# A hybrid decoder block on one core: down projections two output tiles at a time, alternating between their two banks

## The reference, cut to what matters

```
x   = layer_norm(ALPHA * x + mix, ln1_g, ln1_b)
hid = silu(einsum('bsd,df->bsf', x, w_gate)) * einsum('bsd,df->bsf', x, w_up)
ffn = einsum('bsf,fd->bsd', hid, w_down)          # D_FF = 2816, D_MODEL = 1024
x   = layer_norm(ALPHA * x + ffn, ln2_g, ln2_b)
```

## Time and profile before

| | |
|---|---|
| Time, median of 3 runs | 1458.66 us (1458.49 to 1458.88) |
| Time of the profiled execution | 1459.72 us |
| Its span, first to last instruction | 1457.9 us |
| Mean granted clock of TensorE | 0.996 of full speed |
| TensorE busy | 1438.5 us, 99% |
| VectorE, GpSimd, ScalarE busy | 796.0, 601.2, 485.2 us |

### The profile page before, as it was taken

How to read it: one execution, slowest core, us unless ns; L and a number is a source line. 1 busy time by engine, 2 the same in 40 slices (tenths; PEclk the granted TensorE clock), 3 DMA queues, 4 the chain that set the end, 5 groups by cost and what they waited for, 6 DMA issues and landing times. The chain is left out here.

```text
span 1457.9 us, 19033 instructions
## 1 busy us (share of the span) xinstructions
PE 1438.5 (99%) x6658; PEld 1195.1 (82%) x6658; DVE 796.0 (55%) x1196; ACT 485.2 (33%) x933; POOL 601.2 (41%) x374
## 2 busy tenths in 40 slices
PE   9999999999999999999999899999999999999997
PEld 7888888888888888887887688888888888888886
DVE  3126564557457644766866835545345353454547
ACT  4433433343334323334255332312323223232133
POOL 2221122212312231214873484655637547364464
PEclk9999999999999999999999999999999999999999
DMA  6211111111111011011420121212111112112112
GB/s 174 59 44 44 44 29 58 41 31 43 43 43 43 29 51 50 29 43 58 124 79 15 58 73 37 65 43 65 50 44 58 50 58 64 29 60 61 45 51 116
DMA packets 128407, 80.22 MB, mean 55 GB/s; under 512 B 8433, under 2 KB 123121, under 8 KB 128369
## 3 DMA queue, kind: packets, MB, share of 16 engines
q1 hardware_dynamic: 128368, 79.73, 18.2%
HBM read 75.53 MB, written 4.19 MB: 55 GB/s over the span
## 5 line engine op out<-in xcount | busy, mean ns | idle before, releaser
L1341 PE MATMUL ps<-act_hi,w_hi 128*128 128x512 f32 x864 | 339.3, 393 | 1.1 <-DVE act_lo L906 1.1
L476 POOL TENSOR_TENSOR w_lo<-raw,w_hi 128x1024 fp32r<-128x1024 f32 x54 | 131.6, 2437 | 505.3 <-ACT w_hi L616 505.3
L1342 PE MATMUL ps<-act_lo,w_hi 128*128 128x512 f32 x864 | 337.3, 390 | 0.0
L1343 PE MATMUL ps<-act_hi,w_lo 128*128 128x512 f32 x864 | 337.1, 390 | 0.0
L564 POOL TENSOR_TENSOR w_lo<-raw,w_hi 128x512 fp32r<-128x512 f32 x80 | 108.3, 1354 | 227.8 <-ACT w_hi L819 227.8
L1343 PEld LDWEIGHTS ps<-act_hi,w_lo 128*128 128x128 f32 x864 | 162.6, 188 | 34.5
L1341 PEld LDWEIGHTS ps<-act_hi,w_hi 128*128 128x128 f32 x864 | 162.6, 188 | 33.5 <-issue 1.3
L1342 PEld LDWEIGHTS ps<-act_lo,w_hi 128*128 128x128 f32 x864 | 162.8, 188 | 32.1
L1341 PE MATMUL ps<-hid_hi,wd_hi 128*128 128x512 f32 x320 | 125.0, 391 | 4.2 <-DVE res L1184 4.2
L1190 DVE TENSOR_TENSOR res<-res,ps 128x512 f32<-128x512 f32 x128 | 87.9, 687 | 68.3 <-PE ps L1343 67.8
L1343 PE MATMUL ps<-hid_hi,wd_lo 128*128 128x512 f32 x320 | 124.6, 389 | 0.0
(11 more groups left out here) (193 smaller groups left out, 2547.5 us busy)
## 6 DMA issues: line engine op xcount, KB each, us to landing
raw<-in_w_in SPq DMA_DIRECT2D x52, 512.0 KB, 3.8
raw_d<-in_w_down SPq DMA_DIRECT2D x22, 512.0 KB, 3.2
raw<-in_w_gate SPq DMA_DIRECT2D x40, 256.0 KB, 2.8
raw<-in_w_up SPq DMA_DIRECT2D x40, 256.0 KB, 3.1
raw<-in_w_out SPq DMA_DIRECT2D x16, 512.0 KB, 3.6
xs<-in_x SPq DMA_DIRECT2D x8, 512.0 KB, 8.0
out<-rows SPq DMA_DIRECT2D x7, 512.0 KB, 2.6
raw_b<-in_w_gate SPq DMA_DIRECT2D x1, 512.0 KB, 5.1
```

The source lines that it names most:

```text
L476: pool.tensor_tensor(w_lo[:, slot], raw[:, slot], fp(w_hi[:, slot]), ALU.subtract).then_inc(w_lo_s, 1)
L1341: pe.matmul(bank, w_h(t), a_hi(t), start=(t == 0), stop=False)
L1342: pe.matmul(bank, w_h(t), a_lo(t), start=False, stop=False)
L1343: last = pe.matmul(bank, w_l(t), a_hi(t), start=False, stop=(t == tiles - 1))
```

## The change

`down` now makes two output tiles per call, m and m + 1, in their two banks 4 + v % 4 and 4 + (v + 1) % 4. Its twelve matmuls alternate between the two: high x high of the one tile, high x high of the other, high x low of the one, and so on. The two tiles use different weight tiles and the same activations. The last matmul of each tile increments `d_s`, so the increments are those of matmuls 11 and 12 of the twelve. The wait on `add_s` stands ahead of the pair and asks for one add more than that of the even tile did: both banks must be free. The loops that call `down` go in steps of two. VectorE's, ScalarE's, GpSimd's and SyncE's programs are unchanged.

```diff
                 if v >= 4:
-                    pe.wait_ge(add_s, i * 32 + (16 * c + v - 3))
-                product(ps[:, 4 + v % 4, :], lambda t: wd_hi[:, t, blk(m)], lambda t: wd_lo[:, t, blk(m)],
-                        lambda t: hid_hi[:, t, half(h)], lambda t: hid_lo[:, t, half(h)], 2).then_inc(d_s, 1)
-
+                    pe.wait_ge(add_s, i * 32 + (16 * c + v - 2))
+                for t in range(2):
+                    for w, a in ((wd_hi, hid_hi), (wd_hi, hid_lo), (wd_lo, hid_hi)):
+                        for e in range(2):
+                            last = pe.matmul(ps[:, 4 + (v + e) % 4, :], w[:, t, blk(m + e)], a[:, t, half(h)],
+                                             start=(t == 0 and w is wd_hi and a is hid_hi),
+                                             stop=(t == 1 and w is wd_lo))
+                            if t == 1 and w is wd_lo:
+                                last.then_inc(d_s, 1)
...
             for h in range(2):
-                for m in range(DT):
+                for m in range(0, DT, 2):
                     down(0, 0, h, m)
...
                     if c % 2:
-                        for v in range(2 * DT):
+                        for v in range(0, 2 * DT, 2):
                             down(i, (c + 1) // 2, v // DT, v % DT)
...
                 if c == 1:
-                    for v in range(2 * DT):
+                    for v in range(0, 2 * DT, 2):
                         down(last_pairs, 1, v // DT, v % DT)
```

## The result

The changed kernel takes 1461.32 us (median of 16 runs, 1460.28 to 1462.52), the kernel before 1458.74 us (16 runs, 1458.08 to 1460.08). The ratio is 1.0018, 95% interval [1.0011, 1.0024]: 2.6 us more, 0.18%. The forecast was 1460.9, in a range of 1459.0 to 1463.2. The profiled execution spans 1460.4 us, 2.5 more than the one before.

A forecast was written before the change was run, and what follows sets the result against it. The prediction took TensorE, busy 99% of the span, as the bound. It added 1.3 (first block), 0.75 (nine steady blocks) and 0.15 (clock), 2.2 us, to the median 1458.66, giving 1460.9; range 1459.0 to 1463.2.

The forecast's parts named there:

- No price and no gain from alternation: All 960 down matmuls: changing bank at every matmul leaves the spacing at 0.22667 us; effect taken as 0.
- The seams: Where a matmul opens a tile in another bank; in the earlier trace these stood at the usual 0.22667 us pitch.
- The rival with 13.3 ns a matmul: Down matmuls: alternating banks shortens spacing to the bare 512 columns, 12.8 us less, 1448.1 us in all; chance 0.06.
- The steady blocks: Nine later down blocks, T their start: tile 4's load waits for add 1, 0.15 us late; together 0.75 us lost.
- The first block: First down block, paced by VectorE's adds: pairs leave eight tiles instead of seven after the last wait, 1.3 us later.
- The waits forecast: First down block: TensorE waits three times for VectorE's L1184, about 1.6, 3.1 and 1.2 us.
- The clock: First down block: TensorE's clock may halve after a 3.1 us hole; 0.3 us paid at half a chance, 0.15.
- The sum: Whole kernel: first block 1.3, steady blocks 0.75 and clock 0.15 make 2.2 us more, +0.15%.
- The lower end of the range: Whole kernel: 1459.0 us, said to be the sum with both lower ends, with 0.3 allowed for noise.

The follow-up runs named there:

- experiment 4: Changed kernel, matmuls still alternating, but each bank waits only for its own add instead of both; 1460.21 us beside 1458.82, ratio 1.0009.
- experiment 3: Changed kernel with the wait for both banks kept, but the two tiles made in turn without alternation; 1460.56 us beside 1458.82, ratio 1.0011.
- experiment 5: Changed kernel with VectorE's two second-half gate steps ahead of add 0 in the later blocks; 1460.62 us beside 1459.11, ratio 1.0009.
- experiment 1: Kernel before, with pairs in the first down block only; 1460.08 us beside 1458.82, ratio 1.0009.
- experiment 8: Changed kernel with twelve unread matmuls filling the first block's 3.1 us hole; 1461.09 us beside 1459.11, ratio 1.0015.
- experiment 6: Kernel before, with VectorE's adds 2 and 3 moved up in the first block; 1457.40 us beside 1459.11, ratio 0.9984.
- experiment 9: Kernel before, with adds 2 and 3 and also the first depth difference moved up in the first block; 1457.13 us beside 1458.72, ratio 0.9990.

## Why the prediction held, point by point

- **No price and no gain from alternation.** Right. The seams of the earlier trace rows bore it out: 226.67 ns in 96 alternating matmuls (experiment 4). The rival with 13.3 ns a matmul didn't come. Neither did the 216 ns of the Trainium skill (TensorE: Matmul & The Clock Gate, Back-to-back issue gap). That section gives them for single matmuls, and 131 ns for a stream with a weight load each. The trace has a weight load each and 226.67 ns in either order, and disagrees with both.
- **The steady blocks.** Right in mechanism and size. Forecast: add 0 at T+2.70, end of add 1 T+5.31, load T+5.36, 0.07 a block and 0.19 in the last. Measured: the same three places, 0.04 to 0.07 a block, mean 0.057 (0.45 in eight), and 0.20. Experiments 3, 4 and 5 each take away one of its three conditions (late completion, common wait, gate steps between the adds), and each brings 21.76 back (21.79 in the last block of experiment 4).
- **The first block.** Right, but with half of the account. Forecast 1.3 and 0.15 for the clock; measured 1.41, and 1.33 in experiment 1. The prediction puts the loss down to the common wait, and experiment 3 shows that this alone does it. It does not say that the alternating order alone costs nearly the same, 1.16 in experiment 4. What holds the bank closed is the place of the add in VectorE's queue: moving two adds gives back 2.3 us in the one kernel and 2.9 in the other (28.68 to 25.82).
- **The waits forecast** for the first block, 1.6, 3.1 and 1.2 us: the first two came (1.59 and 3.08), the third only where the clock did not fall (1.29 in experiment 8). At half clock, tiles 6 and 7 took longer by about what that wait would have been.
- **The clock.** I gave the fall half a chance. It fell behind the 3.1 us hole in each of the four profiled kernels that have it (the changed one, 1, 3 and 5). It fell in experiment 4 too, behind a hole of 2.2 us that has one matmul and 0.57 us of idle time just ahead of it. In this block it did not fall in the others, whose longest hole is 1.7 us. The Trainium skill (same page, HAM oscillation) has that a TensorE left waiting comes back at half clock, and the traces agree for these longer holes. In the changed kernel it came back at 1.00 (829.5 to 831.2) and fell only then. The price was right in kind: the next wait hides most of it. In size it was 0 to 0.15, where the prediction reckoned 0.3 for a fall that comes. It entered the sum with 0.15 only because half a chance was put on it, and that this fits is luck.
- **The sum.** 2.2 forecast, 2.07 in the blocks, 2.6 between the medians with an interval of 1.6 to 3.5. The median stands 0.18% up, just inside the 0.2% that counted as no change, and the spread of single runs is as large as the effect. The lower end of the range, 1459.0, is not what its own terms give: 1458.66 + 1.2 is 1459.9. Nothing hung on it.

## What to carry to other kernels

A wait that asks for two buffers at once comes true only with the later one. What is lost then is the work that used to run between the two releases: count how many tiles stand behind the last wait. Separate waits do not save it where the order alternates between the two buffers, because the matmuls behind the first closed bank stand too (experiment 4). Completing two tiles together also delays the first of them; look at which queue stands behind its consumer and whether the consumer was waiting. Where an engine is 99% busy, the rest may be another engine's order: here two adds moved in VectorE's queue took 1.7 us off the median, and no order of the matmuls that was tried took off any.

## What the runs showed of the hardware

The spread of the runs is some 2 us in either kernel, and the profiles show where part of it may come from. There are two places ahead of the first down block where the clock falls in some executions: behind an idle stretch that ends at about 684, and at about 783, soon after sixteen one-column matmuls that run from 780.0 to 781.9. Three of the eleven profiled executions have both falls (the kernel before, the changed one and experiment 3), the other eight have one. The second stretch, first in the kernel before, then in experiment 1:

```profile
783.30:786.60 3.30, 3.30 (x9) 2.59 (x8) 0.19 (x2) 0.85 (x2) 0.00 (x0) 0.50 0.35 130
```
```profile
783.30:786.60 3.30, 3.30 (x21) 2.85 (x19) 0.57 (x2) 1.23 (x2) 0.00 (x0) 1.00 0.45 159
```

The program is the same up to there. The first down block then starts at 816.28 in the one and at 815.10 in the other. It starts between 816.18 and 816.74 in the three executions with both falls, and between 814.86 and 816.47 in the eight with one. These differences are as large as what the change costs.

The 0.46 us by which the changed kernel's block started late are not of this kind, since both executions have both falls. They come in earlier, in waits that have nothing to do with the change. At 8 us a product waited longer for an input, first in the kernel before, then in the changed one:

```profile
7.98 1.09 PE L1364 MATMUL ps<-ident,xs 128*128 128x128 f32 x8 [0.38 <-DMA xs<-in_x]
```
```profile
8.30 1.09 PE L1364 MATMUL ps<-ident,xs 128*128 128x128 f32 x8 [0.64 <-DMA xs<-in_x]
```

That is 0.3 us of it. The rest comes in at 684, where TensorE waited 3.09 us for GpSimd's L520 instead of 2.94.

A fall of the clock can also be nearly free: at half rate a pair of tiles took the time that TensorE would have spent waiting (0 to 0.15 us, experiment 8).

A VectorE operation with both tensor operands in SBUF took 1.4 to 1.9 us instead of 0.7 where it started while GpSimd worked (first blocks of the kernel before and of experiments 6 and 9), while the adds that read PSUM kept their 0.68. The end of such an operation follows GpSimd's: at 831.37 + 1.76 = 833.13 it stands 0.55 behind 831.29 + 1.29 = 832.58. In the whole trace of the kernel before, 86 VectorE operations on 512 columns with two tensor operands, both in SBUF, start inside a GpSimd operation. Of these, 78 end 0.55 or 0.56 us behind the end of a GpSimd operation. The other 8 start so late in it that their usual 0.69 us end later than that. An operation that starts first keeps its 0.74 though GpSimd starts within it (829.43; GpSimd at 829.65). So it is the order of the starts that counts. No run here varies GpSimd's part by itself, so this rests on the trace alone.
